# Half of the modulation vectors' weights, in the first feed-forward part, summed on VectorE from transposed strips

## The chip, the cores and the metric

One core of a Trainium2 chip runs the whole kernel. Times are device microseconds (us) of one launch; a profile is one execution, with every instruction's start and duration.

## What is computed

An encoder of two layers over 256 prompt and 32 sample tokens (T = 288) of 2048 features, fp32. Layer 0 is an RWKV-7 mixer and a squared-ReLU feed-forward part; layer 1 is latent attention over one shared key/value latent and another feed-forward part. Every sub-layer is modulated by vectors made from a condition `c` (one row for the prompt, one for the sample):

```python
cs = jax.nn.silu(c)                                   # (1, 2048), for prompt and sample each
mod = (cs @ W['ada_w'][l] + W['ada_b'][l]).reshape(B, N_MOD, D)       # 6 vectors of 2048, per layer
h = modulate(rmsnorm(x, W['norm_mlp_g'][l]), mod[:, 3], mod[:, 4])
x = x + mod[:, 5][:, None, :] * sq_relu_mlp(h, W['mlp_w1'][l], W['mlp_w2'][l])
# the shared latent has two more: cs @ W['kv_ada_w'] + W['kv_ada_b']
```

That makes 14 vectors of 2048 features ("the vectors"): 28672 features, each a sum over 2048 products, for two conditions.

## The kernel before

Activations lie transposed, features on the 128 partitions (16 blocks, KB) and tokens on the free axis. All weights come as one stream of slots of 128x1024 fp32 (512 KB), loaded by SP's queue into the eight buffers of `raw`.

A **product slot** is split: ScalarE copies it to `whi` in a rounded format (L584), VectorE subtracts to get the rest, `wlo` (L999). TensorE then does three matmuls for each of eight 128x128 pieces (`three`, L1651 to L1655), hi x hi, lo x hi, hi x lo, 128x288 each: 24 in a slot. There are SPL = 4 buffers of `whi` and `wlo`, so split j waits until slot j - 4 is used. A **vector slot** isn't split: TensorE takes a column pair of `cs` (silu of the two conditions) as the stationary operand and lets 256 columns of the weights pass, four matmuls to a slot, each on another column group (0, 32, 64, 96) of the array (`ada_slot`, L1627 to L1639).

The work is a row of stages, each of four groups. In a *mixed* stage (r, k, v, o, and m1_0_c and m2_0_c for c = 0 to 3, the first feed-forward part) a group is: four vector slots (a *burst*), four product slots, four vector slots, four product slots. The eight vector slots of a group give 512 features: VectorE copies the sums from PSUM (`row`, L1002), TensorE turns them onto the partitions with four columns of a selecting table (`ada_finish`, L1641), VectorE adds the bias into `mod` (`mods`, L1010). Of 56 such groups, 8 come ahead of stage r (ada0), 16 in r, k, v and o, and 32 in the first feed-forward part; group 24 (counted from 0) is the first of m1_0_0.

Each engine has its own program in its own order, held together by semaphores. `walk` (L388) is that of ScalarE and VectorE for a stage: splits 2 to 7 of the group, the row copy, split 0 of the next group, the epilogue (`epi`) of bank 0, split 1 of the next, the epilogues of banks 1 to 3, `mods`. The epilogue of m1 stages squares the ReLU and splits the result; that of o and m2 stages adds the gated sum to `x` (L1025). SP's program (L444 to L500) loads slots in the stream's order: in mixed stages buffers 0 to 3 hold vector slots (load waits for `ada_used`) and 4 to 7 product slots (load waits for `lo_ready`) (`behind_both`, L461). POOL issues small loads and stores: `xT` and `trig` at the start of stage o (L555, L556), the attention's caches after slot `kvd.q0` (L559 to L563), and outputs, each with a semaphore of its own.

At the start of stage o VectorE waits for both loads of L555 and L556 before slot 2's split (L1435). After m2_0_3 come the norm of the shared latent (N_KV), stages kvd and wdq, then attention (att0, wo0, att1, wo1) and the second feed-forward part, which has no vector slots.

## Time and profile before

| | |
|---|---|
| median of 3 runs | 3544.47 us (3541.55 to 3548.25) |
| the profiled execution | 3541.34 us, span 3539.8 us |
| TensorE busy (matmul) | 3372.5 us, 95% |
| VectorE busy | 1753.8 us, 50% |
| ScalarE busy | 1414.0 us, 40% |
| vector slots' matmuls (L1637) | 3584 records, 228.9 us busy |
| moved by DMA | 664.50 MB, 188 GB/s over the span |

An fp32 matmul of two fp32 operands has two records, one of the rounded format has one. Matmuls are pipelined, so their rows overlap: what one costs is read from the starts of rows, not from their durations. A busy row on VectorE or ScalarE overlaps the next by about 0.1 us in the same way.

### The profile page before, as it was taken

To read this page: it belongs to the slowest core of one execution; us is meant where nothing else is said; L and a number is where in the kernel's file an instruction comes from. 1 tells how busy PE (TensorE), PEld (TensorE's weight loads), DVE (VectorE), ACT (ScalarE), POOL (GpSimd) and SP (SyncE) were. 2 spreads that over 40 slices of the span, in tenths; PEclk is the share of its full clock that TensorE was granted. 3 is DMA by queue.
4 is the path that set the end of the run, shared out by engine and by line. 5 is a ranking of instruction groups with operands and counts; after the bars stand their busy time and mean duration, and the time that the engine had idled before them with its cause. 6 is when DMAs were issued, how large, how long until landed. Compare 5 with 4: busy or idle time off the path is not lost.

```text
span 3539.8 us, 82073 instructions
## 1 busy us (share of the span) xinstructions
PE 3372.5 (95%) x32608; PEld 3110.5 (88%) x32608; DVE 1753.8 (50%) x2931; ACT 1414.0 (40%) x2272; POOL 42.2 (1%) x81
## 2 busy tenths in 40 slices
PE   6899988888899999999999988999998999999998
PEld 2699977777798999999999987899898999999998
DVE  3444436666545444434444465545646544445455
ACT  2333325555435323323333374433435434334342
POOL 0000000000000000000000000000000000000000
PEclk8999999999999999999999999999999999999999
DMA  9777730000376777777777742243244454545543
GB/s 365 268 279 279 280 138 15 17 15 17 145 279 243 282 278 281 285 284 279 278 279 278 278 143 97 94 137 122 89 142 138 156 171 154 172 160 166 166 149 109
DMA packets 181757, 664.50 MB, mean 188 GB/s; under 512 B 21238, under 2 KB 21408, under 8 KB 181056
## 3 DMA queue, kind: packets, MB, share of 16 engines
q1 hardware_dynamic: 178272, 652.28, 51.3%
q0 software_dynamic: 3296, 9.48, 0.9%
q8 instruction: 146, 2.39, 0.3%
q14 instruction: 43, 0.35, 0.0%
HBM read 657.58 MB, written 4.09 MB: 187 GB/s over the span
## 4 chain that ended last, share of the span: by engine, by line
PE 91%; DVE 3%; DMA 2%; ACT 2%; issue 2%; SPq 0%; DVEq 0%; POOL 0%; ACTq 0%; POOLq 0%
PE ps L1653 24%; PE ps L1655 23%; PE ps L1654 23%; PE ps L1762 6%; PE ps L1637 5%; PE ps L1769 2%; DMA sb_raw<-stream 1%; PE ps L2046 1%; PE ps L2048 1%; PE ps L2047 1%; PE ps L1734 1%; PE ps L2079 1%; PE ps L2078 1%; PE ps L1647 1%; ACT sb_whi L584 1%
## 5 line engine op out<-in xcount | busy, mean ns | idle before, releaser
L999 DVE TENSOR_TENSOR sb_wlo<-sb_raw,sb_whi 128x1024 fp32r<-128x1024 f32 x778 | 940.7, 1223 | 1104.2 <-ACT sb_whi L584 1089.4
L584 ACT ACTIVATE sb_whi<-sb_raw 128x1024 fp32r<-128x1024 f32 x778 | 811.8, 1057 | 1268.7 <-PE ps L1655 619.9
L1653 PE MATMUL ps<-sb_ah,sb_whi 128*128 128x288 f32 x3728 | 1116.2, 299 | 34.5 <-DVE sb_al L1097 17.9
L1654 PE MATMUL ps<-sb_ah,sb_wlo 128*128 128x288 f32 x3728 | 1103.2, 296 | 0.0
L1655 PE MATMUL ps<-sb_al,sb_whi 128*128 128x288 f32 x3728 | 1099.4, 295 | 0.0
L1653 PEld LDWEIGHTS ps<-sb_ah,sb_whi 128*128 128x128 f32 x3728 | 702.2, 188 | 68.5 <-issue 54.1
L1655 PEld LDWEIGHTS ps<-sb_al,sb_whi 128*128 128x128 f32 x3728 | 705.4, 189 | 0.0
L1654 PEld LDWEIGHTS ps<-sb_ah,sb_wlo 128*128 128x128 f32 x3728 | 703.7, 189 | 0.1
L1653 PE MATMUL ps<-sb_bh,sb_whi 128*128 128x288 f32 x2048 | 609.6, 298 | 2.3 <-DVE sb_x L1025 2.3
L1654 PE MATMUL ps<-sb_bh,sb_wlo 128*128 128x288 f32 x2048 | 604.1, 295 | 0.0
L1655 PE MATMUL ps<-sb_bl,sb_whi 128*128 128x288 f32 x2048 | 602.1, 294 | 0.0
L1653 PEld LDWEIGHTS ps<-sb_bh,sb_whi 128*128 128x128 f32 x2048 | 383.6, 187 | 17.0 <-issue 13.5
L1655 PEld LDWEIGHTS ps<-sb_bl,sb_whi 128*128 128x128 f32 x2048 | 385.6, 188 | 0.0
L1654 PEld LDWEIGHTS ps<-sb_bh,sb_wlo 128*128 128x128 f32 x2048 | 384.5, 188 | 0.0
L1637 PE MATMUL ps<-sb_raw,sb_cs 128*2 128x256 f32 x3584 | 228.9, 393 | 30.5 <-DMA sb_raw<-stream 24.1
L1637 PEld LDWEIGHTS ps<-sb_raw,sb_cs 128*2 128x2 f32 x3584 | 81.0, 84 | 135.4 <-DMA sb_raw<-stream 39.1
L1025 DVE SCALAR_TENSOR_TENSOR sb_x<-ps,sb_mod,sb_x 128x256 f32<-128x256 f32 (+1 forms) x352 | 104.8, 359 | 121.6 <-PE ps L1655 121.4
L605 ACT ACTIVATE sb_work<-ps 128x288 f32<-128x288 f32 x128 | 51.4, 402 | 125.6 <-PE ps L1655 107.5
L1033 DVE TENSOR_TENSOR sb_work<-sb_work 128x288 f32<-128x288 f32 x128 | 58.0, 453 | 82.8 <-ACT sb_work L605 82.7
L1298 DVE COPY_PREDICATED sb_p<-sb_con,ps 128x320 f32<-128x320 uint32 x96 | 49.2, 513 | 76.5 <-PE ps L1762 76.5
L731 ACT ACTIVATE sb_yt<-ps 128x320 f32<-128x320 f32 x80 | 35.0, 437 | 98.2 <-PE ps L1762 96.7
L1762 PE MATMUL ps<-sb_yt,sb_p 64*64 64x64 f32 x1600 | 63.4, 219 | 10.0 <-ACT sb_yt L731 9.2
(276 smaller groups left out, 3246.7 us busy)
## 6 DMA issues: line engine op xcount, KB each, us to landing
sb_raw<-stream SPq DMA_DIRECT2D x1226, 512.0 KB, 5.4
sb_x<-xT SPq DMA_DIRECT2D x1, 2304.0 KB, 15.7
sb_x<-xT POOLq DMA_DIRECT2D x1, 2304.0 KB, 9.7
yT<-sb_x SPq DMA_DIRECT2D x4, 576.0 KB, 2.8
sb_lwa<-lw POOLq DMA_DIRECT2D x16, 130.0 KB, 2.7
sb_lwg<-lw POOLq DMA_DIRECT2D x16, 130.0 KB, 2.4
sb_l1g<-l1g SPq DMA_DIRECT2D x2, 1024.0 KB, 20.0
wkvT<-sb_st POOLq DMA_DIRECT2D x16, 64.0 KB, 2.4
```

Of the source, the lines that this page charges most:

```text
L584: nc.scalar.activation(whi[:, q % SPL, :], raw[:, n % RAW, :], ACT.Copy).then_inc(hi_ready, 1)
L605: nc.scalar.activation(work[:, m % 2, :], PS[:, m, 0:T], ACT.Relu).then_inc(bank_free[m], 1)
L999: nc.vector.tensor_tensor(wlo[:, q % SPL, :], raw[:, n % RAW, :], whi[:, q % SPL, :], ALU.subtract).then_inc(lo_ready, 1)
L1025: ins = nc.vector.scalar_tensor_tensor(out=xb, in0=PS[:, m, cols], scalar=flat(mod[:, bass.ds(4 * it + (KB * s.gate + m), 1), z:z + 1]), i ...
L1033: nc.vector.tensor_tensor(work[:, 2 + m % 2, :], work[:, m % 2, :], work[:, m % 2, :], ALU.mult).then_inc(hid_sq, 1)
L1298: nc.vector.copy_predicated(t[f"p{l}"][:], const(MASK_L + C * l).bitcast(mybir.dt.uint32), chunks(PS[:, 4 * u + 3, 0:TT])).then_inc(m["q"], 1)
L1637: ins = mm(PS[g:g + 2, 4, 0:256], cs[:, 2 * p + j, :], raw[:, n % RAW, a:a + 256], start=p == 0, stop=p == 7)
L1653: mm(out, wh, xh, start=start, stop=False)
L1654: mm(out, wl, xh, start=False, stop=False)
L1655: return mm(out, wh, xl, start=False, stop=stop)
L1762: ins = mm(PS[p, 4 * u + bank, C * c:C * c + C], lhs(p, c), rhs(p, c), start=opens is None or (opens and c == 0), stop=opens is None)
L1769: ins = mm(PS[p, 4 * u + q // 4, P * (q % 4):P * (q % 4) + P], lhs[p, c], rhs[p, c].rearrange("p a t -> p (a t)"), start=True, stop=True)
```

## The change

From the second group of m1_0_0 on (31 groups) only one burst of four vector slots is left in a group. It holds 256 features instead of 512: a slot is now 4 blocks of the sum by 256 columns (`by_burst`), its four matmuls again on column groups 0, 32, 64, 96, and `half_finish` adds the four partial rows with two other columns of the table. The other 256 features of each group (blocks 162 to 223 of `mod`, the last 62 of 224) come from `strips`: their weights transposed, features on the partitions and half of the 2048 terms (1024) on the free axis; 124 strips of 512 KB. POOL's queue loads them into two buffers. `crow` holds the two conditions' rows on all partitions; VectorE multiplies a strip with half a row and sums it along the free axis by the accumulator's output, once per condition: 8 instructions in a group, after splits 2 to 7 by 2, 1, 1, 2, 1, 1. The first of the two writes its products into PSUM banks 6 and 7, the second onto the strip. At the end of m2_0_3 two instructions add the halves and the bias.

In stage o POOL waits for x, then loads crow and the first two strips; ScalarE and VectorE make silu of crow in group 1 (four instructions of 1024 each). `trig` moves behind the last strip, and VectorE no longer waits for it in stage o. SP's loads of the 31 groups follow a new order (`behind_half`). The stages of m1_0_0 are written out for its four groups. Several semaphores are merged (`cache_in` with `rows_in`; `ckv_out`, `kpe_out` and `last_out` become `pool_out`), so that ScalarE and VectorE wait at those places for all loads or stores of the set.

```diff
+HALVED = BY["m1_0_0"].ada0 + 1
+HALF_GROUPS = 8 * 4 - 1
+HALF0 = 4 * HALVED
+STRIP0 = HALF0 + 2 * HALF_GROUPS
+STRIPS = 4 * HALF_GROUPS
+STRIP_PLACES = (2, 1, 1, 2, 1, 1)
+HALVED_AT = BY["m1_0_0"].n0 + 2 * RAW
...
                 elif make is None:
                     for j in range(s.hoist, s.per):
                         split(s, j, it)
+                        if beside is not None:
+                            beside(s, it, j - s.hoist)
...
+            def behind_half(g):
+
+                for i in range(BURST):
+                    sp.wait_ge(lo_ready, 2 * BURST * g + (BURST * (HALVED_AT // RAW - 2 - VECTORS) - 2 * BURST + i + 1))
+                    fetch(g * 12 + (HALVED_AT - 16 + i), BURST + i)
+                    sp.wait_ge(ada_used, BURST * g + (ADA_FULL - 2 * BURST + i + 1))
+                    fetch(g * 12 + (HALVED_AT - 12 + i), i)
+                for i in range(BURST):
+                    sp.wait_ge(lo_ready, 2 * BURST * g + (BURST * (HALVED_AT // RAW - 2 - VECTORS) - BURST + i + 1))
+                    fetch(g * 12 + (HALVED_AT - 8 + i), BURST + i)
...
             pool.dma_start(x[:], d["xT"]).then_inc(x_back, 16)
+            pool.wait_ge(x_back, 16)
+            pool.dma_start(crow[:], d["crow"].partition_broadcast(P)).then_inc(x_back, 16)
+            for k in range(2):
+                pool.dma_start(strip[:, k, :], d["strips"][k]).then_inc(strip_in[k], 16)
+            with pool.Fori(1, STRIPS // 2) as i:
+                for k in range(2):
+                    pool.wait_ge(strip_used, i * 4 + (2 * k - 2))
+                    pool.dma_start(strip[:, k, :], d["strips"][bass.ds(i * 2 + k, 1)].rearrange("a p c -> (a p) c")
+                                   ).then_inc(strip_in[k], 16)
+            pool.wait_ge(strip_used, 2 * STRIPS)
             pool.dma_start(trig[:], d["trig"]).then_inc(x_back, 16)
...
-            act.wait_ge(S["cache_in"], 16)
+            act.wait_ge(S["cache_in"], 112)
...
-            act.wait_ge(S["ckv_out"], 16)
+            act.wait_ge(pool_out, 64)
...
+            def row_sigmoid(s, it, i):
+
+                if it == 1 and i < 4:
+                    if i == 0:
+                        act.wait_ge(x_back, 32)
+                    z, a = i // 2, HS * (i % 2)
+                    nc.scalar.activation(csig[:, z, a:a + HS], crow[:, z, a:a + HS], ACT.Sigmoid).then_inc(c_sig, 1)
...
+            def strip_sums(s, it, i):
...
+                for e in range(sum(STRIP_PLACES[:i]), sum(STRIP_PLACES[:i + 1])):
+                    k, z = e // 2, e % 2
+                    if z == 0:
+                        dve.wait_ge(strip_in[k % 2], it * 32 + 16 * (2 * g + k // 2 + 1))
+                        done = 8 * g + e - 1
+                        if not isinstance(it, int) or 8 * it + done > 0:
+
+                            dve.wait_ge(strip_used, 8 * it + done)
+                    w = strip[:, k % 2, :].rearrange("p (a t) -> p a t", a=2)
+                    nc.vector.scalar_tensor_tensor(
+                        out=w if z else PS[:, 6:8, :], in0=w, scalar=1.0,
+                        in1=crow[:, z, HS * (k % 2):HS * (k % 2) + HS].rearrange("p (a t) -> p a t", a=2),
+                        op0=ALU.mult, op1=ALU.mult,
+                        accum_out=flat(parts[:, bass.ds(2 * it + (2 * g + k // 2), 1), 2 * (k % 2) + z:2 * (k % 2) + z + 1])
+                        ).then_inc(strip_used, 1)
...
-            dve.wait_ge(x_back, 32)
+            dve.wait_ge(x_back, 16)
             gemm("o", "m1_0_0")
...
+            def half_slot(s, it, p):
+
+                pe.wait_ge(landed[p], it * 16 + 16 * (s.ada0 + (HALVED_AT // RAW + 1 - HALVED)))
+                if p == 0:
+
+                    pe.wait_ge(arow_ready, s.ada0 + it)
+                for z in range(4):
+                    ins = mm(PS[32 * z:32 * z + 2, 4, 0:256], cs[:, 4 * p + z, :], raw[:, p, 256 * z:256 * z + 256],
+                             start=p == 0, stop=p == BURST - 1)
+                ins.then_inc(ada_used, 1)
+
+            def half_finish(g):
+
+                pe.wait_ge(arow_ready, g + 1)
+                pe.wait_ge(mod_ready, g)
+                for m in range(2):
+                    ins = mm(PS[:, 5, 2 * m:2 * m + 2], arow[:, P * m:P * m + P], con[:, SEL + 4:SEL + 6],
+                             start=True, stop=True)
+                ins.then_inc(ada_fin, 1)
...
                 def group(it):
+                    half = s.mixed and halved(s, it)
                     for p in range(8):
-                        if s.mixed and p % BURST == 0:
+                        if half and p == 0:
+                            for a in range(BURST):
+                                half_slot(s, it, a)
+                        elif s.mixed and not half and p % BURST == 0:
                             for a in range(BURST):
                                 ada_slot(s, it, p + a)
                         gemm_slot(s, it, p, xh, xl)
-                    if s.mixed:
+                    if half:
+                        half_finish(s.ada0 + it)
+                    elif s.mixed:
                         ada_finish(s.ada0 + it)
```

## Rows read from the trace of the kernel before

**Rows 1.** Page, the span in 40 slices: TensorE's busy tenths, granted clock.

```profile
PE   6899988888899999999999988999998999999998
PEclk8999999999999999999999999999999999999999
```

**Rows 2.** Page, the chain that ended last, by engine.

```profile
PE 91%; DVE 3%; DMA 2%; ACT 2%; issue 2%; SPq 0%; DVEq 0%; POOL 0%; ACTq 0%; POOLq 0%
```

**Rows 3.** Stretch (length, busy PE, PEld, DVE, ACT, POOL; clock, DMA share, GB/s); wait, 1090 to 2045.

```profile
1084.00:2044.00 960.00, 959.87 (x8287) 884.75 (x8287) 423.63 (x606) 338.72 (x439) 0.00 (x0) 1.00 0.75 279
...
ACT sb_whi L584 <- DMA sb_raw<-stream: 538.2, 145, 10.5
```

**Rows 4.** The chain in order of time: start, us, what; the bursts of one group.

```profile
1324.67 1.84 PE ps L1637 x32
1339.48 1.84 PE ps L1637 x32
...
1354.65 1.84 PE ps L1637 x32
```

**Rows 5.** TensorE in order of time: start, duration, line, output<-inputs, count.

```profile
1309.20 0.29 PE L1655 MATMUL ps<-sb_bl,sb_whi 128*128 128x288 f32 x1
...
1311.50 0.29 PE L1654 MATMUL ps<-sb_bh,sb_wlo 128*128 128x288 f32 x1
...
1326.93 0.29 PE L1653 MATMUL ps<-sb_ah,sb_whi 128*128 128x288 f32 x1
...
1338.92 0.29 PE L1653 MATMUL ps<-sb_ah,sb_whi 128*128 128x288 f32 x1
```

**Rows 6.** VectorE's groups by form (busy us, mean ns); stretch of one squared-ReLU group.

```profile
L999 DVE TENSOR_TENSOR sb_wlo<-sb_raw,sb_whi 128x1024 fp32r<-128x1024 f32 x778 | 940.7, 1223 | 1104.2 <-ACT sb_whi L584 1089.4 <-DMA sb_trig<-trig 8.7 <-issue 0.3
L1025 DVE SCALAR_TENSOR_TENSOR sb_x<-ps,sb_mod,sb_x 128x32 f32<-128x32 f32 x96 | 23.2, 242 | 0.0
L1111 DVE SCALAR_TENSOR_TENSOR sb_mx<-sb_xx,sb_vec,sb_hb 128x288 f32<-128x288 f32 x48 | 22.9, 515 | 6.6 <-PE ps L1734 6.3
...
1354.60:1384.60 30.00, 30.00 (x265) 27.62 (x268) 13.54 (x19) 11.59 (x17) 0.00 (x0) 1.00 0.75 280
```

**Rows 7.** ScalarE in attention, in order of time: accumulator read-out and next instruction.

```profile
2181.25 0.19 ACT L897 ACTIVATION_READ_ACCUMULATOR sb_pr<-ps,sb_mxs 128x1 f32 x1
2181.34 0.47 ACT L899 ACTIVATE sb_pr<-ps,sb_mxs 128x256 f32<-128x256 f32 x1
```

**Rows 8.** VectorE in order of time: the first two splits behind an epilogue.

```profile
1358.44 2.36 DVE L999 TENSOR_TENSOR sb_wlo<-sb_raw,sb_whi 128x1024 fp32r<-128x1024 f32 x2
```

**Rows 9.** DMA issues (KB each, us to landing): 1084 to 2044; then 2040 to 2150.

```profile
sb_raw<-stream SPq DMA_DIRECT2D x507, 512.0 KB, 7.0
...
sb_raw<-stream SPq DMA_DIRECT2D x22, 512.0 KB, 3.3
sb_vt<-cckv POOLq DMA_DIRECT2D x1, 256.0 KB, 3.2
```

**Rows 10.** POOL and ScalarE in order of time, behind the first feed-forward part.

```profile
2046.10 1.99 POOL L563 DMA_DIRECT2D sb_qp<-qrow  x4
2126.53 0.57 POOL L569 DMA_DIRECT2D kpeT<-sb_kpe  x1
...
2079.03 0.61 ACT L831 ACTIVATE sb_kyh<-sb_vt 128x512 fp32r<-128x512 f32 x1
```

**Rows 11.** Start of stage o by engine, [idle before <-releaser]; x's landing.

```profile
948.50 0.54 POOL L555 DMA_DIRECT2D sb_x<-xT  x1 [6.69 <-DVEq L1374]
960.20 2.36 DVE L999 TENSOR_TENSOR sb_wlo<-sb_raw,sb_whi 128x1024 fp32r<-128x1024 f32 x2 [8.70 <-DMA sb_trig<-trig]
961.48 0.40 PE L1653 MATMUL ps<-sb_ah,sb_whi 128*128 128x288 f32 x1 [2.02 <-DVE sb_wlo L999]
965.17 1.06 ACT L584 ACTIVATE sb_whi<-sb_raw 128x1024 fp32r<-128x1024 f32 x1 [13.23 <-DMA sb_raw<-stream]
...
sb_x<-xT POOLq DMA_DIRECT2D x1, 2304.0 KB, 9.7
```

More of the change, by code:

```diff
@@ L72 @@
 SEL = CARRY + TT
-NCONST = SEL + 4
+NCONST = SEL + 6
 LW_W, LW_A = 0, P
@@ L378, in bank_wait, with halved, place @@
                 eng.wait_ge(slot_used, s.per * it + (s.q0 + s.per))
+        def halved(s, it):
+            return s.ada0 + (it if isinstance(it, int) else 1) >= HALVED
+        def place(s, j):
+            n = s.at(j)
+            skipped = HALF_GROUPS if n >= BY["kvd"].n0 and n % RAW < BURST else 0
+            return n % RAW, n // RAW + 1 - skipped
         def value_bank(h):
@@ L386, in reader_done, with walk @@
             eng.wait_ge(slot_used, s.q0 + (s.groups - 1) * s.per + p + 1)
-        def walk(eng, s, nxt, split, produce, epi, row, mods, lead=None, early=None, sums=None):
+        def walk(eng, s, nxt, split, produce, epi, row, mods, lead=None, early=None, sums=None, beside=None):
             def group(it, after, make=None):
@@ L1057, in gemm @@
             def gemm(name, nxt, produce=None, lead=None, early=None):
-                walk(dve, BY[name], nxt, split, produce, epi, row, mods, lead, early, sums if name in NORM_OF else None)
+                walk(dve, BY[name], nxt, split, produce, epi, row, stage_mods, lead, early,
+                     sums if name in NORM_OF else None, row_silu if name == "o" else strip_sums if BY[name].mixed and BY[name].ada0 + 1 >= HALVED else None)
             def inverse_root(i, root=None):
@@ L2272 @@
                 h = halves(w)
-                g = 32 * (2 * c + j)
-                parts.append(woven(later[g:g + 32], h) if layer == 0 else h)
+                if layer == 0:
+                    if not c + j:
+                        parts.append(woven(first, h[:8]))
+                        h = h[8:]
+                    g = max(8 * c + 4 * j - 1, 0)
+                    h = h.reshape(-1, 8, P, HS)
+                    h = np.concatenate([bursts[g:g + len(h)], h], 1).reshape(-1, P, HS)
+                parts.append(h)
         if layer:
@@ L2314 @@
         "cT": np.stack([column(a["c_prompt"][0]), column(a["c_sample"][0])], -1),
+        "crow": np.stack([a["c_prompt"][0], a["c_sample"][0]]), "strips": strips(later[:, cut:]),
         "con": constants(), "vec": vec, "lw": lw, "s0": s0,
```

130 lines of the change are left out of this document (91 added, 39 removed).

## The prediction

> **What bounds the kernel now.** I read the slices of the page first. From the eleventh slice of forty on, TensorE is full; the stretch in question is about slices 13 to 23, with the clock at its upper level (2.4 GHz) [rows 1]. The chain that ended last is 91% TensorE [rows 2]. Then the stretch table: from 1084 to 2044 us, where the eight stages of the first feed-forward part run (32 groups), TensorE is busy 959.87 of 960 us and VectorE 423.63 [rows 3]. So time comes off here only by taking work off TensorE, as long as VectorE, ScalarE and the transfers keep ahead. The list of who waited for whom says what is ahead of what: the longest wait in the stretch is ScalarE's for landing weights, 538.2 us in 145 pieces [rows 3], and TensorE does not stand in the list. Such waits are those of an engine that runs ahead of TensorE, since a split may be at most four slots ahead of its use.
>
> A group is two bursts of four vector slots (32 matmul records each) and eight product slots. In the chain's list the bursts start at 1324.67, 1339.48 and 1354.65: 14.81 and 15.17 us apart, 29.98 a group; the odd 0.36, at the group's end, is `ada_finish` [rows 4]. Product matmuls start 0.1332 us apart (90 from 1326.93 to 1338.92, 11.99 us), so four product slots of 24 are 12.79 us [rows 5]. The rest of 14.81 is the burst: **2.02 us**. Read directly it is the same: without the burst the matmul of L1654 that starts at 1311.50 would have started two pitches after 1309.20, at 1309.47; 2.03 us [rows 5].
>
> **The change on TensorE.** 31 of the 32 groups (all but the first of m1_0_0) lose one of two bursts. The one that stays has again 16 matmuls of 256 columns on the four column groups 0, 32, 64, 96, so it should cost 2.02. `half_finish` still loads two weight tiles and writes fewer columns: I keep its 0.36. Nothing else of TensorE's is touched. 31 x 2.02 = **62.6 us** off, a group of 27.96 us, if all else keeps up.
>
> **VectorE, per group.** It gets eight `scalar_tensor_tensor` of 128x1024 fp32 with an accumulator output (248 in all). The trace has none of that kind; the bounds: the same instruction without accumulator on two SBUF operands takes 515 ns for 288 elements, and 242 ns for 32, thus 1.07 ns an element and 515 + 736 x 1.07 = 1.30 us for 1024; a plain subtraction of 1024 is 1.223 us [rows 6]. The accumulator's read-out exists on ScalarE only: a row of 0.2 us, which moves the next instruction by 0.09 us [rows 7]. So 1.22 us below and 1.30 + 0.22 = 1.52 above; I take 1.4, near the upper of the close rows, since one of each pair waits for the one before it. A far bound comes with the rivals. Eight are 11.2 us. Today VectorE is busy 13.54 us of a squared-ReLU group, the fuller kind [rows 6]; with 11.2 more, 24.7 of 27.96. It fits in sum; in order it must also fit in place. From the start of the burst: today the epilogue and `mods` are done and split 2 starts at +3.8 (1358.44 against 1354.65) [rows 4, 8]. Then, at 1.13 us a split (two in 2.36) and 1.4 a strip sum, in the order of STRIP_PLACES: split 2 ready at +4.9, two sums to +7.7, split 3 +8.8, sum +10.2, split 4 +11.3, sum +12.7, split 5 +13.9, two sums +16.7, split 6 +17.8, sum, split 7 +20.3, sum +21.7, the row copy, the next group's split 0 at +23.2. TensorE wants slot p at 2.02 + 3.20p: 8.4, 11.6, 14.8, 18.0, 21.2, 24.4 for slots 2 to 7. The smallest cover is 2.8 us (slot 3). The next fixed point is bank 0, at +25.4: VectorE has 2.2 us left over. So I cost the sums at nothing; if the cover is gone, every microsecond beyond it is paid 31 times.
>
> **Strips.** Bytes stay the same: four strips of 512 KB replace four vector slots of a group. They move from SP's queue to POOL's, with two buffers. By the schedule above buffer 0 is free at +7.7 and wanted at +13.9 (6.2 us), buffer 1 free at +12.7 and wanted at +17.8 (5.1 us). No 512 KB load of POOL's is in the trace: 256 KB took 3.2 us, and SP's 512 KB took 3.3 us behind the part and 7.0 us (median) in it, where up to eight stand in line [rows 9]. At 3.3 nothing waits; at 7.0 the first wait is 0.8 and the second 1.1 us, 1.9 together, still within 2.2. What is queued behind a late strip on VectorE is the next split; who waits for that is TensorE, after 2.8 us of cover. POOL's program has nothing else between L556 and L559. DMA runs at 279 GB/s with a share of 0.75 [rows 3]; the same bytes in 27.96 instead of 29.98 us need 0.80.
>
> **SP's queue.** A product load now stands behind a vector load that waits for TensorE's burst. The latest is product 7's: it goes out when split 3 is ready (+8.8), with a vector load and a strip in line at most (1.41 us each at 279/0.75 GB/s [rows 3]), and is wanted at +14.8, when slot 3 is done: 6.0 us for 3.3 + 2 x 1.41 = 6.1, and VectorE wants it 3 us after that; free. The vector slots have a whole group to land. The semaphore merges are free too: the last of the seven cache loads is issued by 2048.1 and ScalarE uses the first at 2079.03; kpeT goes out at 2126.5 and, with a landing of some 3 us, is done by 2130, while the query latent's product, norm and split still stand between it and the first wait [rows 9, 10]. The final sum over 62 blocks is two instructions of 124 elements per partition with VectorE ahead of TensorE.
>
> **Stage o.** VectorE today waits there for the table trig: x lands at 948.50 + 9.7 = 958.2, VectorE goes on at 960.20, and TensorE waits 2.02 us [rows 11]. Now it waits for x alone: up to 2.0 us gained. Against it crow (2 MB over all partitions) and two strips (1 MB) start at 958.7. Product slot 4 landed at 965.17 there [rows 11]; with 1.06 + 1.22 for its split it is ready at 967.5. TensorE wants it two slots and a burst after slot 2's start, at 961.48 + 2 x 3.20 + 2.02 = 969.9: 2.4 us of cover, 0.4 once TensorE is 2 us earlier. x, on POOL's queue beside SP's, got 2.36 MB in 9.7 us, 243 GB/s, more than half of 372 [rows 3, 11]; so slot 4 may land 1 us later or, if all bytes ahead of it share, up to 6.5. Bounds: 2.0 gained to 5 lost; I take 1.0 gained, as most of slot 4's bytes are ahead of crow. The four sigmoids (a table load or two with them) and four products of 1024 in group 1 come to about 4.2 and 4.9 us on engines that idle over half of a group (13.54 of 30 and 11.59 of 30 busy [rows 6]) and lie ahead of TensorE; nothing.
>
> **Sum.** 3541.34 (profiled execution; its span 3539.8) - 62.6 - 1.0 = 3477.7. The median of the runs is 3.1 above that execution, so 3480.8; I say **3481**.
>
> **Rivals.** *A, the forecast*: TensorE stays the bound, 3481. Chance 0.72.
>
> *B, slower: VectorE becomes the bound because the accumulating instruction reads two fp32 operands at half the rate.* Place: each of the 248 sums. Price: 242 + 992 x 2.13 = 2.36 us. Then VectorE needs 13.54 + 8 x 2.36 = 32.4 us a group by busy rows, or 30.7 if each of the 19 instructions overlaps the next by 0.09 (1.223 against a pitch of 1.13 [rows 6, 8]); middle 31.6, 1.6 more than today: 31 x 1.6 = +50, 3594. It turns into a loss from (29.98 - 11.8)/8 = 2.3 us a sum by the pitch, 2.1 by the busy rows. Against it: L1111, two fp32 SBUF operands, runs at full rate [rows 6]; for it: no row has an accumulator. Chance 0.10. The Trainium skill, Vector Engine (DVE) Microarchitecture Reference, "Points that are easy to get wrong", states this rule for two sources that are not bf16, giving the missing port for the accumulator's readback as reason. The trace disagrees for the form without accumulator (1.07 ns an element) and has no row with it; by the rule the sum would be B's, by the rows A's.
>
> *C, part of the gain: strips come late or the sums are near 1.8 us.* With landings of 9 to 11 us from POOL's queue the waits go beyond the 2.2 us left over; for 1 us a group too much 31 us of the gain are lost: 3512. For it: two buffers only and 5.1 us; against: beside a strip SP has one or two loads in line here, not eight. Chance 0.14. The Trainium skill, SBUF — State Buffer, "SBUF: two separate sides", warns that loads issued by GpSimd wait for descriptors while VectorE runs an instruction in a two-port mode; what VectorE runs here are two-operand instructions, and no row here has both together.
>
> *D: the saving is eaten elsewhere* (crow's traffic stalls more than bounded, or the burst left behind grows): within 0.2% of 3544. Chance 0.04.
>
> **How the numbers follow.** Faster by over 0.2% (about what a measurement of this kernel can tell from no change): A and C, 0.86; same: D and the edge of B, 0.04; slower: B, 0.10. The range holds A and most of C: low 3474 (the full 2.0 in stage o, and 5 us of scatter), high 3525; B is left out.
>
> **What would show it.** In the changed profile: bursts 27.96 us apart in each group, 12.79 + 12.79 + 2.02 + 0.36; TensorE busy through the stretch with no wait for `sb_wlo`; rows of the strip sums at 1.3 to 1.5 us and a read-out beside each; VectorE's waits for `sb_strip` below 2 us a group; POOL's queue with some 67 MB more. Wrong would be: sums of 2.3 us and TensorE waiting for `sb_wlo` in each group (B), strip landings above 8 us (C), a wait over 5 us between 958 and 975 (D).

## The result and the profile after

The changed kernel took 3498.82 us (median of 4 runs, 3496.72 to 3501.44), the kernel before 3543.84 beside it (4 runs, 3541.55 to 3548.25): a ratio of 0.9872, 95% interval 0.9855 to 0.9889. That is 45 us off, where the sum of the prediction has 63.6. The profiled execution took 3496.72 us, its span is 3495.2 (3541.34 and 3539.8 before). So two questions stand: did the steady groups give what was forecast, and where did the other 18.6 us go?

The page of the changed kernel first: span, busy times, and POOL's queue (packets, MB, share), which now carries the strips.

```profile
span 3495.2 us, 80783 instructions
PE 3316.4 (95%) x31616; PEld 3091.3 (88%) x31616; DVE 2036.0 (58%) x3433; ACT 1419.5 (41%) x2278; POOL 108.1 (3%) x206
...
q0 software_dynamic: 21296, 76.60, 6.6%
```

The stretch of the halved groups, in the table by stretches (us, busy us of each engine, granted clock, DMA share, GB/s), and bursts from the chain in order of time (start, us, what):

```profile
1114.00:1980.00 866.00, 865.96 (x7052) 831.13 (x7052) 676.74 (x1061) 320.60 (x406) 63.97 (x121) 1.00 0.82 298
```

```profile
1128.29 1.84 PE ps L1765 x32
...
1883.38 1.84 PE ps L1765 x32
```

TensorE is busy 865.96 of 866 us. From 1128.29 to 1883.38 lie 27 groups in 755.09 us: 27.97 each, where 27.96 was forecast; the same 27 took 809.64 before. The longest stretch has given all of it. What is missing must lie at the seams. The waits from 940 to 2100 us (who waited, for whom: us in total, times, longest), first VectorE's for strips, then TensorE's for blocks of the norm's result (`sb_al`):

```profile
DVE ps L1112 <- DMA sb_strip<-strips: 93.7, 55, 4.0
...
PE ps L1790 <- DVE sb_al L1214: 13.9, 2, 8.2
```

To place the loss I took marks that every kernel has (starts of bursts and of first products in TensorE's rows) and measured between them. A: from the first burst of stage o to that of its third group. B: to the last burst of stage o. C: on through the norm to the first product of m1_0_0. D: to the end of its first group, which keeps both bursts (the first burst of group 25; for before the same place). E: the next 27 groups. F: three more. G: on to the first product of stage kvd. All in us, each from one profiled execution:

| kernel | A | B | C | D | E | F | G | sum |
|---|---|---|---|---|---|---|---|---|
| before | 64.11 | 44.81 | 26.09 | 30.56 | 809.64 | 89.96 | 40.23 | 1105.40 |
| after | 68.38 | 44.80 | 27.21 | 39.55 | 755.09 | 83.90 | 42.40 | 1061.33 |
| e1, queue order | 66.52 | 44.81 | 26.73 | 30.85 | 755.09 | 83.91 | 40.44 | 1048.35 |
| e2, crow later | 65.15 | 44.81 | 26.28 | 41.06 | 755.09 | 83.90 | 41.61 | 1057.90 |
| e3, table early | 66.66 | 44.81 | 26.22 | 40.92 | 755.09 | 83.90 | 42.93 | 1060.53 |
| e4, third buffer | 67.42 | 44.80 | 26.61 | 41.01 | 755.09 | 83.90 | 38.23 | 1057.06 |
| e5, no strips | 62.51 | 44.80 | 25.75 | 41.61 | 755.09 | 83.90 | 38.22 | 1051.88 |
| e9, all, spread | 63.61 | 45.37 | 26.23 | 30.14 | 755.09 | 83.90 | 38.22 | 1042.56 |

Before to after: A +4.3, C +1.1, D +9.0, E -54.6, F -6.1, G +2.2 where the last saved burst should have given -2.0. The sum is -44.1, and outside the marks the two executions agree within 0.5 us (2434.4 and 2433.9). So the four seams are A, C, D and G.

**Seam D, 9.0 us.** Rows of the changed kernel there: ScalarE, VectorE, TensorE and SP's queue (start, us, what, [idle before and who ended it]) and the transfers by tens of us:

```profile
1109.07 1.06 ACT L639 ACTIVATE sb_whi<-sb_raw 128x1024 fp32r<-128x1024 f32 x1 [10.77 <-DMA sb_raw<-stream]
...
1110.16 1.23 DVE L1063 TENSOR_TENSOR sb_wlo<-sb_raw,sb_whi 128x1024 fp32r<-128x1024 f32 x1 [11.11 <-ACT sb_whi L639]
...
1103.42 1.91 PE L1754 MATMUL ps<-sb_raw,sb_cs 128*2 128x256 f32 x32
1113.57 0.58 PE L1790 MATMUL ps<-sb_ah,sb_whi 128*128 128x288 f32 x1 [8.24 <-DVE sb_al L1214]
...
1104.25 7.64 SPq L483 DMA_DIRECT2D sb_raw<-stream  x9
```

```profile
1090.00:1100.00 10.00, 10.00 (x67) 10.00 (x67) 7.17 (x15) 8.14 (x18) 0.00 (x0) 0.87 0.03 9
...
1110.00:1120.00 10.00, 6.43 (x38) 6.46 (x39) 7.96 (x15) 9.47 (x21) 0.00 (x0) 0.67 0.98 389
```

From 1090 to 1100 hardly a byte moves (share 0.03), ScalarE has waited 10.77 us when a product slot lands, some 4 us after TensorE's second burst (1103.42), and TensorE stands for 8.24. (Its row names `sb_al`, because on ScalarE and VectorE the norm's next block stands behind that slot's split.) The weights did not wait for bandwidth, they waited for their turn: SP issues a load at 1084.32 and the next at 1104.25, 0.8 us into the second burst. In `behind_half` the loads of product slots 5 to 7 of group 24 stand behind vector loads of group 25, and each of those waits for a matmul of that second burst to free its buffer. In steady groups the same order costs nothing (27.97 us a group); group 24 alone has a second burst. Theory 1: D is SP's order of issue.

**Seam A, 4.3 us.** Again ScalarE and TensorE, then five-microsecond stretches:

```profile
968.37 1.06 ACT L639 ACTIVATE sb_whi<-sb_raw 128x1024 fp32r<-128x1024 f32 x1 [17.27 <-DMA sb_raw<-stream]
...
948.28 3.59 PE L1754 MATMUL ps<-sb_raw,sb_cs 128*2 128x256 f32 x32 [4.11 <-DVE ps L1548]
...
965.53 1.91 PE L1754 MATMUL ps<-sb_raw,sb_cs 128*2 128x256 f32 x32
...
970.74 0.61 PE L1790 MATMUL ps<-sb_ah,sb_whi 128*128 128x288 f32 x1 [3.30 <-DVE sb_wlo L1063]
...
986.67 1.91 PE L1754 MATMUL ps<-sb_raw,sb_cs 128*2 128x256 f32 x32
```

```profile
965.00:970.00 5.00, 2.44 (x37) 1.10 (x35) 0.54 (x1) 1.06 (x1) 0.00 (x0) 0.98 0.96 389
970.00:975.00 5.00, 4.26 (x18) 4.26 (x19) 2.33 (x3) 2.35 (x3) 0.00 (x0) 0.50 1.02 408
975.00:980.00 5.00, 5.00 (x34) 5.00 (x34) 2.36 (x3) 0.82 (x1) 0.00 (x0) 0.84 1.03 411
```

The start gained 1.71 us as argued (first burst to second: 17.25 against 949.12 to 968.08, 18.96, before). Then slot 4 is late and TensorE waits 3.30; behind the wait the granted clock is 0.50 for five microseconds and 0.84 for five more. The gap of 21.14 to the next burst, 15.17 without a stall, is the wait and 2.7 us that go with the half clock. Theory 2: crow and two strips (3 MB, POOL, from 957.92) share the transfers with slot 4.

**Seam G, 4.2 us.** VectorE's waits for strips in the last stage, m2_0_3, where the loads run out of time, then TensorE at the end:

```profile
1930.97 1.23 DVE L1112 SCALAR_TENSOR_TENSOR ps<-sb_strip,sb_crow 128x1024 f32<-128x1024 f32 x1 [3.23 <-DMA sb_strip<-strips]
...
1959.59 1.23 DVE L1112 SCALAR_TENSOR_TENSOR ps<-sb_strip,sb_crow 128x1024 f32<-128x1024 f32 x1 [3.41 <-DMA sb_strip<-strips]
```

```profile
1995.03 0.50 PE L1774 MATMUL ps<-sb_con,sb_arow 128*128 128x2 f32 x4
...
2009.61 0.58 PE L1790 MATMUL ps<-sb_ah,sb_whi 128*128 128x288 f32 x1 [6.61 <-issue]
```

These two sums start 28.62 us apart (the next one 28.60 later), while TensorE's bursts stay 27.97 apart: VectorE falls behind by 0.6 us a group, unseen, because TensorE has slots in hand. In the four groups of m2_0_3 this sum starts 19.0, 19.7, 20.3 and 21.0 us behind its group's burst, so a good part of the delay is there in the first of them. It is paid at the norm, where TensorE wants the epilogue itself: from the last finish to kvd's first product 14.58 us. Theory 3: a third buffer mends it.

**Seam C, 1.1 us.** The sigmoids of stage o change ScalarE's table, and the norm's square root must load its own again: a row that the kernel before does not have in this place.

```profile
1080.80 1.28 ACT L687 ACT_TABLE_LOAD   x1
1082.09 0.50 ACT L687 ACTIVATE sb_work<-ps,sb_eps 128x288 f32<-128x288 f32 x1
```

### The profile page after: what moved, and what is told of

Read it like the earlier page. It is cut to its first block, busy times and chain, and to the rows that moved or that the text cites. A ratio compares the mean times of both kernels' runs of the same rounds, so it can differ in the third digit from the quotient of the medians.

```text
span 3495.2 us, 80783 instructions
## 1 busy us (share of the span) xinstructions
PE 3316.4 (95%) x31616; PEld 3091.3 (88%) x31616; DVE 2036.0 (58%) x3433; ACT 1419.5 (41%) x2278; POOL 108.1 (3%) x206
## 4 chain that ended last, share of the span: by engine, by line
PE 88%; DVE 4%; DMA 3%; issue 2%; ACT 2%; SPq 0%; DVEq 0%; ACTq 0%; POOLq 0%
PE ps L1790 23%; PE ps L1792 22%; PE ps L1791 22%; PE ps L1905 6%; PE ps L1754 2%; DMA sb_raw<-stream 2%; PE ps L1912 2%; PE ps L1765 1%; PE ps L2189 1%; PE ps L2191 1%; PE ps L2190 1%; DVE sb_wlo L1063 1%; PE ps L1877 1%; ACT sb_whi L639 1%; DMA sb_strip<-strips 1%
## 5 line engine op out<-in xcount | busy, mean ns | idle before, releaser
L1112 DVE SCALAR_TENSOR_TENSOR ps<-sb_strip,sb_crow 128x1024 f32<-128x1024 f32 x124 | 152.5, 1230 | 93.7 <-DMA sb_strip<-strips 93.7
L1112 DVE SCALAR_TENSOR_TENSOR sb_strip<-sb_strip,sb_crow 128x1024 f32<-128x1024 f32 x124 | 151.3, 1220 | 0.0
L1754 PE MATMUL ps<-sb_raw,sb_cs 128*2 128x256 f32 x1600 | 112.5, 416 | 28.9 <-DMA sb_raw<-stream 22.5
L1754 PEld LDWEIGHTS ps<-sb_raw,sb_cs 128*2 128x2 f32 x1600 | 35.2, 85 | 88.6 <-DMA sb_raw<-stream 39.0
L610 POOL DMA_DIRECT2D sb_strip<-strips x122 | 64.5, 529 | 957.9 <-DVE sb_strip L1112 942.8
```

The costliest lines, as they stand in the source:

```text
L610: pool.dma_start(strip[:, k, :], d["strips"][bass.ds(i * 2 + k, 1)].rearrange("a p c -> (a p) c")).then_inc(strip_in[k], 16)
L1112: nc.vector.scalar_tensor_tensor(out=w if z else PS[:, 6:8, :], in0=w, scalar=1.0, in1=crow[:, z, HS * (k % 2):HS * (k % 2) + HS].rearrang ...
L1754: ins = mm(PS[g:g + 2, 4, 0:256], cs[:, 2 * p + j, :], raw[:, n % RAW, a:a + 256], start=p == 0, stop=p == 7)
```

## The experiments

All times come beside runs of the kernel before on the same chip. e1 to e4 have one run each (before beside them 3549.05).

**e1, order of SP's queue.** Group 24's last eight product loads go out ahead of the vector loads of group 25; from the next group on all is as it was.

```
+            for i in range(BURST):
+                sp.wait_ge(lo_ready, BURST * (HALVED_AT // RAW - 2 - VECTORS) + i + 1)
+                fetch(HALVED_AT - 4 + i, BURST + i)
+            for i in range(BURST):
+                sp.wait_ge(ada_used, ADA_FULL - BURST + i + 1)
+                fetch(HALVED_AT + i, i)
...
-            with sp.Fori(1, HALF_GROUPS + 2) as g:
+            with sp.Fori(2, HALF_GROUPS + 2) as g:
```

> Only the order of SP's loads behind the last full group (24) is changed: product slots 4 to 7 of group 24 are loaded ahead of group 25's vector slots, instead of between them. Theory (queue): product slots 5 to 7 of group 24 stood behind a vector load that waits for TensorE's second burst of that group; group 24, from its first product matmul to group 25's burst, took 39.62 us in the changed kernel against 30.63 in the one before, and will take 30.6 here, the whole 9.0 us less. Rival (DMA): the slots land late because the transfers of crow and the strips crowd the stretch; then the order alone gives under 2 us and group 24 stays at 37 us or more.

Measured: 3483.53 us; D is 30.85 us (39.55). Its bursts:

```profile
1099.96 1.91 PE L1763 MATMUL ps<-sb_raw,sb_cs 128*2 128x256 f32 x32
...
1115.12 1.91 PE L1774 MATMUL ps<-sb_raw,sb_cs 128*2 128x256 f32 x32
```

They are 15.16 us apart, a half group with nothing lost (24.8 in the changed kernel, from 1103.42). With the same bytes, the same strips and another order the stall is gone: theory 1 stands. 8.7 of the 9.0 us are SP's order, and in e10, the same kernel again, D is 29.61.

**e2, crow later.** Crow is loaded after the eighth slot of stage o, and its silu made a group later.

```
+            pool.wait_ge(slot_used, BY["o"].q0 + 8)
             pool.dma_start(crow[:], d["crow"].partition_broadcast(P)).then_inc(x_back, 16)
...
-                if it == 1 and i < 4:
+                if it == 2 and i < 4:
```

> crow and the first two strips are loaded after stage o's first group, and crow's silu is made in group 2 instead of 1. Theory (transfers): 3 MB from POOL's queue, beside SP's loads, delay product slot 4 and what follows; from stage o's first vector burst to group 21's first burst the changed kernel took 38.46 us against 34.19 before. Without them 2.0 us less than before, for VectorE no longer waits for trig: 32.2. Rival: the delay comes from SP's own loads (the six in line behind x), and the stretch stays above 37; second rival: the 3 MB cost the same 4 us one group later.

Measured: 3498.08 us. TensorE's bursts in stage o, and its wait between the last two of them:

```profile
965.96 1.91 PE L1755 MATMUL ps<-sb_raw,sb_cs 128*2 128x256 f32 x32
...
981.13 1.91 PE L1755 MATMUL ps<-sb_raw,sb_cs 128*2 128x256 f32 x32
995.95 1.91 PE L1755 MATMUL ps<-sb_raw,sb_cs 128*2 128x256 f32 x32
...
1000.52 0.40 PE L1791 MATMUL ps<-sb_ah,sb_whi 128*128 128x288 f32 x1 [2.67 <-DVE sb_wlo L1064]
...
1013.85 1.91 PE L1755 MATMUL ps<-sb_raw,sb_cs 128*2 128x256 f32 x32
```

The stall after the second burst is gone (15.17), so it was crow's and the strips'; but 995.95 to 1013.85 is 17.90, 2.7 over. The load was moved, and nearly the whole wait moved with it: 2.67 us against 3.30. The price is 2.7 instead of 6.0 us because here the clock does not fall behind the wait (granted 1.00 from 1000 to 1010). e11 has the same edit; there TensorE waits 2.85 us in this place, the clock does fall, and the gap is 19.59 us, 4.4 over. So moving crow by itself gains little.

**e3, the square root's table early.** One small square root right behind the sigmoids, so that the table load falls where ScalarE idles.

```
                     nc.scalar.activation(csig[:, z, a:a + HS], crow[:, z, a:a + HS], ACT.Sigmoid).then_inc(c_sig, 1)
+                    if i == 3:
+                        nc.scalar.activation(lroot[:, 0:1], eps[:, 0:1], ACT.Sqrt)
```

> One more instruction of ScalarE, a square root of one element per partition behind the last sigmoid of crow. Theory (table): the sigmoids leave another activation table behind, and its reload (a row of 1.28 us) stands in the norm between stage o and m1_0_0; from the last burst of stage o to the first product matmul of m1_0_0 the changed kernel took 27.13 us, the one before 26.02. With the table loaded in group 1, 26.0, and nothing lost in group 1. Rival: the norm is late for another reason (VectorE's own backlog): 27.1 stays.

Measured: 3503.77 us. The norm's square root comes again as in the kernel before, 0.84 us behind TensorE and with no load ahead of it:

```profile
1080.43 0.50 ACT L689 ACTIVATE sb_work<-ps,sb_eps 128x288 f32<-128x288 f32 x1 [0.84 <-PE ps L1854]
```

C as a whole can't decide this: it is 26.22 here, and 26.28 in e2, which has the load. Its last part can, from the first burst of m1_0_0 to its first product: 7.15 or 7.16 us in the seven kernels with the load (after, e1, e2, e4, e6, e7, e10), 6.69 in the five without (e3, e5, e9, e11, e12), 6.82 before. The table costs 0.46 us, not 1.1; the rest of C varies by 1.0 us among kernels that are alike there. e3 is the slowest of these four, though its sum between the marks is 0.8 us below the changed kernel's: 6.8 us more lie behind kvd's first product (last section), where nothing is edited.

**e4, a third buffer** for the last 16 strips, in memory that is free by then.

```
+        third = sb("third", [P, HS], "K", 2 * KB * T * 4)
+        LAST0 = STRIPS - 16
...
-            with pool.Fori(1, STRIPS // 2) as i:
+            with pool.Fori(1, LAST0 // 2) as i:
...
+            for n in range(LAST0, STRIPS):
+                b = strip_place(n)[0]
```

> A third strip buffer in m2_0_3 alone, in 4 KB per partition that are free there. Theory (late strips): from group 52's burst to the first product matmul of kvd the changed kernel took 126.23 us, 4.2 more than the 122.04 that four groups of 27.96 and what was there before would give; VectorE waits 2.9 to 3.4 us in each group for the third or fourth strip, which m2_0_3 has no room for, since it also sums squares. With a third buffer those waits go and the stretch takes 122.0 to 122.5. Rival (VectorE is full): its instructions alone are too many in m2_0_3; the waits for strips shrink but the stretch stays above 125.

Measured: 3496.37 us; G is 38.23 us (42.40). No wait for a strip is left in the rows of m2_0_3, and TensorE at the end:

```profile
1996.99 0.50 PE L1796 MATMUL ps<-sb_con,sb_arow 128*128 128x2 f32 x4
...
2007.68 0.58 PE L1812 MATMUL ps<-sb_ah,sb_whi 128*128 128x288 f32 x1 [6.62 <-issue]
```

10.69 us from the last finish instead of 14.58, and 10.68 in the kernel before: theory 3 stands. In e4's last group the fourth strip's sum starts 16.4 us behind the burst instead of 21.0, and VectorE waits for TensorE again before the epilogue:

```profile
1994.79 0.64 DVE L1163 SCALAR_TENSOR_TENSOR sb_x<-ps,sb_mod,sb_x 128x256 f32<-128x256 f32 x2 [1.30 <-PE ps L1814]
```

This row stands 25.3 us behind the burst, the changed kernel's 28.6 with no wait before it. That is 3.2 of the 4.2 us; the rest falls in the norm and isn't traced further.

**e5, no strips at all.** Everything of the strips' side is left out and the blocks are set to zero by one instruction; the rest stays.

```
-            pool.dma_start(crow[:], d["crow"].partition_broadcast(P)).then_inc(x_back, 16)
-            for k in range(2):
-                pool.dma_start(strip[:, k, :], d["strips"][k]).then_inc(strip_in[k], 16)
...
+                if s.name == "m2_0_3" and i == len(STRIP_PLACES) - 1 and it == 3:
+                    nc.vector.memset(mod[:, STRIP0:STRIP0 + STRIPS // 2, :], 0.0).then_inc(mod_ready, 1)
+                return
```

> Left out of the changed kernel: crow and the strips are neither loaded nor summed, and the blocks of the vectors that they give are set to zero; SP's queue, the bursts and everything else stay. It shows what the whole of the strips' side costs together. If the three losses named so far are the strips' doing or the queue's, each shows in its own place: from stage o's first burst to that of the next group about 32 us (the changed kernel 38.4), as crow and the strips no longer share the transfers there; the stretch from the last vector burst of the first feed-forward part to the first product of stage kvd 38.2 us (42.4), as no strip can be late; group 24 still 39 to 41 us, as the queue's order does that and not the strips. The rival for group 24, strips' traffic in front of the weights, expects about 31 us there. Steady groups: 27.97 us in any case. Time: 3498.8 - 6.4 - 4.2 = about 3488 us, by the rival 3479.

Measured: 3488.81 us, beside before at 3542.85 (median of 9 runs, this and the next three kernels). A is 62.51, G 38.22, D still 41.61. Each seam answers as named: A and G are the strips' side (5.9 and 4.2 us), D is not. A also shows the gain at the start of stage o alone: 64.11 - 62.51 = 1.6 us, within the bound of 2.0.

**e6 and e7, how much VectorE has left.** Two, or six, more multiplications of 128x1024 in each halved group.

```
+                    if z == 1 and k < 3:
+                        for j in range(2):
+                            nc.vector.scalar_tensor_tensor(
+                                out=more[:], in0=crow[:, 0, 0:HS], scalar=1.0, in1=crow[:, 1, 0:HS],
+                                op0=ALU.mult, op1=ALU.mult).then_inc(c_sig, 1)
```

> The changed kernel with two more multiplications of 128x1024 (two fp32 operands in SBUF, no accumulator) on VectorE in each group with strips, after strips 0 and 1. A steady group has VectorE busy 676.7 of 866 us, 21.9 of 27.97 a group, so 6.1 us are idle; two more of 1.14 to 1.23 us are 2.3 to 2.5 us. If the cover of the prediction (2.8 us before slot 3 and 2.2 at the group's end, at 1.4 us a sum; more with sums of 1.14) is about right, the steady group stays 27.97 us and the time at 3498 to 3503. If VectorE is already at its limit through waits in place, the group is 28.5 us or more and the time 3514 or more. If a two-operand fp32 instruction ran at half rate without an accumulator, the rows would be 2.1 us or more.

> As with two more, but with six more multiplications in each group with strips, two after each of strips 0 to 2: 6.8 to 7.4 us of VectorE. By sum that is 21.9 + 6.8 to 7.4 = 28.7 to 29.3 us of work for a group that TensorE does in 27.97: VectorE becomes the bound, a steady group is 28.7 to 30 us, and the 31 groups cost 23 to 63 us more: 3522 to 3562 us, TensorE waiting for the split weights in each group. The rival, that most of VectorE's busy rows overlap their neighbours (pitch 1.14 against 1.23), expects a group still within 0.2 us of 27.97 and less than 3506 us.

Measured: e6 3498.03 us, 27 groups in 755.09: two more cost nothing. e7 3556.08 us, 27 groups in 799.26, 29.60 each: slower than the kernel before the change. VectorE's groups by form in e7 (1200 to 1900 us: busy us, mean ns | idle before), who waited there, and bursts from e7's chain:

```profile
L1122 DVE SCALAR_TENSOR_TENSOR sb_more<-sb_crow 128x1024 f32<-128x1024 f32 x142 | 173.8, 1224 | 2.4
L1113 DVE SCALAR_TENSOR_TENSOR ps<-sb_strip,sb_crow 128x1024 f32<-128x1024 f32 x95 | 116.5, 1227 | 0.0
```

```profile
PE ps L1797 <- DVE sb_wlo L1064: 26.3, 12, 2.4
```

```profile
1487.69 1.84 PE ps L1772 x32
...
1515.72 1.84 PE ps L1772 x32
```

Now VectorE has no idle time before its sums (0.0) and TensorE waits for `sb_wlo`, which never happens in the changed kernel's steady groups. The groups with the residual epilogue are mostly 28.03 us (shown), those with the squared ReLU 30.1 and more. A pair of the added multiplications takes 2.40 us there (start to start), so six are 7.2, and without them VectorE's round would be 20.8 and 22.9 us, against TensorE's 27.97. This is rival B's mechanism, called up on purpose: it decides once VectorE's group grows by 5.1 us, or 0.6 us for each of the eight sums, so at sums of 1.8 us, the value named with rival C.

**e9, all four mended.** e1, e3 and e4 together, with crow loaded in halves after the fourth and twelfth slot of stage o and the strips after the twentieth.

```
+            for z in range(2):
+                pool.wait_ge(x_back, 16 + 16 * z)
+                pool.wait_ge(slot_used, BY["o"].q0 + 4 + 8 * z)
+                pool.dma_start(crow[:, z, :], d["crow"][z].partition_broadcast(P)).then_inc(x_back, 16)
+            pool.wait_ge(slot_used, BY["o"].q0 + 20)
```

> The whole change with its four losses taken out: the product loads of group 24 go out in the order of their use, ahead of the vector loads of group 25; crow is loaded in two halves after the fourth and twelfth slot of stage o and the strips after the twentieth; the row's sigmoids come one group later, with the square root's table loaded right behind them; the last 16 strips have a third buffer. If the losses were rightly named: stage o's first two groups 62.1 to 62.4 us (68.4), group 24 30.6 to 30.9 us (39.6), the stretch from the last burst to kvd's first product 38.2 us (42.4), steady groups 27.97; in all 18 to 20 us less than the changed kernel, 3479 to 3481 us, which is what the prediction's sum came to (3481). If the transfers only stall one group later, as with crow moved by a few slots, 3 to 4 us of stage o stay lost: 3483 to 3484 us.

Measured: 3485.89 us (5 runs, 3485.69 to 3487.41), ratio to before 0.9836 (0.9823 to 0.9850). D and G are as expected, A 63.61 and B 45.37 together 1.7 us over e5's: smaller pieces still stall a little. Between the marks it is 18.8 us shorter than the changed kernel, as expected, but the time misses the expected 3479 to 3481, for the span is only 10.6 us shorter: 1.9 more lie ahead of stage o, and from kvd's first product to the end it takes 1491.9 us, the changed kernel 1485.6, with nothing edited in either place.

**e10, e11, e12: is that the execution or the kernel?** e10 is e1 again, e12 is e9 again, word for word; e11 is e1 to e4 together.

> The kernel with only group 24's loads in order again, word for word, to see how much of a total is the stretch after the first feed-forward part. In the profiles so far that stretch (from kvd's first product to the end) took 1485.3 us in the kernel before, 1485.6 in the changed one, 1487.4 in this kernel's first run and 1491.9 in the spread one, with the same instructions; the difference sits in two places, about 270 and 540 us after kvd's first product, where TensorE idles 2.4 to 2.9 us and the granted clock then either stays 1.00 or falls to 0.50. If that is a matter of the execution, the dips of this kernel's profile differ from its first (0.84 and 0.66 in the five-microsecond pieces behind the idle), and the total moves by up to 6 us: 3481 to 3487. If it is a matter of the kernel, they are the same and the median is 3483.5 within 1. Group 24 30.85 us and the steady groups 27.97 in either case.

> Group 24's loads in order, crow's load after the eighth slot of stage o, the square root's table right behind the sigmoids, the third strip buffer for the last 16 strips: the four edits tried one by one, now together. If they add up (group 24 -8.7, stage o's first two groups -3.2, the norm -0.9, the last stretch -4.2, against the changed kernel's profile), the stretch from stage o's first burst to kvd's first product is 1061.3 - 17.0 = 1044.3 us, and the time 3481.8 where the clock does not dip 270 and 540 us after it, up to 3488 where it does. The rival, that each edit only hands its stall on to the next, expects more than 1050.

> The spread kernel again, word for word. Its own stages should give 1042.6 us from stage o's first burst to kvd's first product, as the first time. If the clock's fall to 0.50 at 270 and 540 us after kvd's first product belongs to the execution, it is gone or smaller in this profile, with 1486 to 1488 us from there to the end (1491.9 the first time); if it belongs to the kernel's own pattern of work, it is there again, with 1490 to 1492, and the median is again 3486 within 1.

Measured, 4 runs each, beside before at 3544.61: e10 3488.90, e11 3488.10, e12 3482.82 us (ratio 0.9820, 0.9804 to 0.9837). e11 took 1045.15 us between the marks (1044.3 expected), so the four edits add up in the sum; term by term they do so only roughly, as A is 67.16 where 65.2 was expected (see e2) and C and D are each 0.6 below. From kvd's first product to the end: e10 1487.3 (e1 1487.4), e12 1491.3 (e9 1491.9), e11 1492.0, with the same falls of the clock in the same places as their twins. Two pairs speak for this part belonging to the kernel; they don't prove it. The medians don't follow it alone: e10 lies 5.4 us above e1's single time, with 5.5 us more ahead of stage o in its profile (951.74 against 946.21), and e12 lies 3.1 below e9. Differences of 3 to 6 us between two single runs of this kernel mean nothing; that is why the verdicts above rest on the marks.

The totals say less than the marks. The changed kernel's ratio is 0.9855 to 0.9889, e9's and e12's lie wholly below it, and e12's four runs all lie below e10's. But e10 (0.9827 to 0.9860) and e11 (0.9816 to 0.9852) can't be told from each other: there, what three more edits add to e1's shows in the marks alone.

The profiles of all runs also say how firm each seam is. D is 39.6 to 41.6 us in the seven kernels with the changed order and 29.6 to 30.9 in the five with e1's. G is 40.4 to 42.9 in the six with two strip buffers (45.9 in e7) and 38.2 in the five with a third or with no strips. A is 66.5 to 68.6 in the seven that load crow at the start of stage o, and 62.5 with no crow and no strips. So each cause is clear of the spread, but the prices read from one profile (9.0, 5.9, 4.2) are good to 1 or 2 us only.

## Why the prediction came out as it did

**The group, 27.96 us: right** (27.97), and with it 60.6 of the 62.6 us, in E and F; the last burst's 2.0 are in G, under what G lost. The burst's price had been read in two ways [rows 4, 5], and both hold.

**The sums, 1.4 us in 1.22 to 1.52: below the estimate, inside the bounds.** VectorE's forms from 1100 to 1980 us, and rows of one group, the first of them POOL's issue of the strip that is summed behind it:

```profile
L1112 DVE SCALAR_TENSOR_TENSOR ps<-sb_strip,sb_crow 128x1024 f32<-128x1024 f32 x122 | 150.0, 1230 | 90.8 <-DMA sb_strip<-strips 90.8
...
L1112 DVE DVE_READ_ACCUMULATOR ps<-sb_strip,sb_crow (+1 forms) x122 | 17.3, 142 | 0.0
```

```profile
1524.93 0.53 POOL L610 DMA_DIRECT2D sb_strip<-strips  x1 [11.36 <-DVE sb_strip L1112]
...
1531.98 1.23 DVE L1112 SCALAR_TENSOR_TENSOR ps<-sb_strip,sb_crow 128x1024 f32<-128x1024 f32 x1 [1.32 <-DMA sb_strip<-strips]
1533.13 0.14 DVE L1112 DVE_READ_ACCUMULATOR ps<-sb_strip,sb_crow 128x1 f32 x1
1533.13 1.22 DVE L1112 SCALAR_TENSOR_TENSOR sb_strip<-sb_strip,sb_crow 128x1024 f32<-128x1024 f32 x1
```

The read-out starts with the next instruction and moves nothing: sums follow one another in 1.15 us, close to a subtraction's 1.13. The lower bound, the subtraction's 1.223 us [rows 6], was the right row; ScalarE's read-out [rows 7] was not. Rival B fell with this: 1.230 us, not 2.36. The rule of the Trainium skill (Vector Engine (DVE) Microarchitecture Reference, "Points that are easy to get wrong") that two such sources halve the throughput is not what this form shows here, nor what e7's form without accumulator shows (1.224 us).

**VectorE's cover: right, and cautious.** Forecast were 2.2 us left over at 1.4 us a sum, which at 1.15 is 4.2; e7 shows 5.1 in the fuller kind of group.

**Strips' waits, 1.9 us a group at a landing of 7.0: too low in steady state, wrong at the end.** In the group of the rows above they are 1.32 and 1.39 us, 2.7 together, and the 90.8 us of the row above come to 3.0 a group, more than the 2 us named as a sign; what VectorE had left over covers that. The last sum on the buffer ends at 1524.27, and the next one on it starts at 1531.98, 7.7 us later: the landing is the forecast's 7.0, but POOL's issue in front of it, 0.7 us behind the sum, had been left out. In m2_0_3 the waits are 3.2 and 3.4 us at one place alone, VectorE's groups become 28.6 us, and rival C's mechanism does act, in the last stage. The step that failed is the test itself: I asked whether VectorE could still be in time for bank 0, and not what it would owe at the norm, where TensorE has no slot in hand. 4.2 us, paid once, not 31 times. The warning of the Trainium skill (SBUF — State Buffer, "SBUF: two separate sides") that GpSimd's loads wait while VectorE is in a two-port mode has no trace here: with VectorE busy 78% of this stretch, POOL's loads land as fast as SP's. Whether any instruction of VectorE's here is in such a mode the rows don't say. Issues from 1100 to 1980 us (KB each, median us to landing):

```profile
sb_raw<-stream SPq DMA_DIRECT2D x380, 512.0 KB, 5.4
sb_strip<-strips POOLq DMA_DIRECT2D x121, 512.0 KB, 5.5
```

**SP's queue, "free": the step that failed, 9.0 us.** I worked out the latest load of a steady group (product 7, cover 6.0) and took that group for all. The order is new, and its first turn meets a group that still has two bursts: there the vector loads ahead of product slots 5 to 7 wait until TensorE has worked through those very products. A queue's order has to be walked through the transition from the old order to the new one, not only round the loop (e1).

**Stage o, -1.0 in -2.0 to +5: right bounds, wrong value.** The gain is there (1.6 us, e5). Slot 4 was to land 1 us later at the least, or up to 6.5 if all bytes ahead of it share, and I took the low end. It came 4.0 us later: ScalarE takes it up 20.71 us behind x's issue (947.66 to 968.37), 16.67 before. With 4.0 the sum's own cover of 0.4 gives a wait of 3.6; 3.30 was measured. From 965 to 975 the DMA share is 0.96 to 1.02, so there was nothing to spare. The other 2.7 of the 5.9 us are half clock behind the wait, a term that the sum didn't have.

**The four sigmoids, "nothing": 0.46 us.** The table load was counted on the way to the sigmoid but not on the way back to the square root. The Trainium skill (ScalarE: Activation LUTs, "What ACT_TABLE_LOAD costs") gives 1283 ns for the load and another 1380 ns of drain. The row agrees with the first (1.28 us); no drain stands in this trace, the square root starts 0.01 us behind the load, and of the load most is hidden under TensorE's part of the norm.

**The semaphore merges, free: right; the final sum, free where VectorE is in time.** Outside the marks before and after agree within 0.5 us. The final sum lies in G: with a third buffer G is 38.22 us, as with no sums at all, but in the changed kernel its two instructions (0.5 us) stand on VectorE's late path.

The forecast of 3481 was thus 17.8 us too low: D 9.0, A 4.3 instead of -1.0 (5.3), G 4.2, the table 0.5, which is 19.0, as is 3496.72 less the sum's 3477.7 for the profiled execution; the median lies 2.1 us above that execution, where 3.1 had been added. The mechanism of the forecast is right, but that the time lies inside the range is in part luck. The range reached that far because of rival C, whose mechanism costs 4.2 us here instead of 31. The largest loss came from a queue for which no rival stood, and crow's traffic, named in rival D, stayed below D's sign (a wait of 3.30 us, not 5). With the seams mended the kernel reaches 3482.8 to 3488.1 (medians of e12, e9 and e11).

## What to carry to other kernels

Taking work off the engine that bounds pays in full in the loop; what it loses is lost at the seams: the first group under a new queue order, the place where new data is first loaded, and the last group before a stage that needs the helper engine's result at once. For each queue whose order changes, write out one turn of the old order followed by one of the new, and look for a load that waits for the very work it is to feed. Where a helper falls behind by less than its lead, nothing shows until the lead is called in; so compare its own period with the loop's, not only who waits for whom.

## What I had not expected of the hardware

A pause of the same length costs nothing in one kernel and nearly 3 us in another. After kvd's first product, at the same instructions, TensorE works 13.07 of 16 us in before, after, e1, e9 and e12. Four-microsecond stretches around the pause (us, busy us of PE, PEld, DVE, ACT, POOL, granted clock, DMA share, GB/s); first after, then e1, then e9:

```profile
2279.61:2283.61 4.00, 2.42 (x16) 2.04 (x14) 2.08 (x6) 3.46 (x9) 0.00 (x0) 1.00 0.00 0
2283.61:2287.61 4.00, 2.91 (x22) 2.91 (x23) 3.31 (x3) 2.62 (x3) 0.00 (x0) 1.00 0.44 138
```

```profile
2264.56:2268.56 4.00, 1.33 (x9) 1.01 (x7) 2.70 (x6) 3.54 (x7) 0.00 (x0) 0.93 0.02 4
2268.56:2272.56 4.00, 4.00 (x21) 4.00 (x22) 2.14 (x2) 1.45 (x2) 0.00 (x0) 0.65 0.68 197
```

```profile
2266.71:2270.71 4.00, 2.51 (x10) 2.51 (x11) 3.50 (x3) 3.02 (x4) 0.00 (x0) 0.60 0.37 102
2270.71:2274.71 4.00, 4.00 (x20) 4.00 (x19) 0.00 (x0) 0.34 (x1) 0.00 (x0) 0.55 0.86 287
```

Behind the pause the clock stays at its upper level (2.4 GHz) in before and after; it goes to the lower one (1.2 GHz) for part of a stretch in e1, e4 and e10, and for most of two in e2, e3, e9, e11 and e12. The same happens once more 270 us later in all of these. e7 has no fall, e5 one short one, e6 a long and a short one. From the end of this pause to the end of a pause of 7.25 us further on, the time goes with the falls: 368.0 or 368.1 us with none (before, after, e7), 369.5 with one short, 370.9 with two short, 372.0 with a long and a short, 373.5 or 373.6 with two long. A short fall costs 1.5 us and a long one 2.8. The tail is 1485.3 and 1485.6 us in the first set, 1487.1 to 1487.4 in the second and 1490 to 1492 in the third, which takes 6.3 of the 18.8 us that e9 saves ahead of it. Two kernels run twice fell alike both times, though the marks lay up to 6.8 us apart; what decides it I can't say from these runs.
